# An attention block whose score mask and softmax division move to VectorE, beside a busy GpSimd

## What the reference computes

```python
s = scale * q @ k.T                     # 768 tokens: 512 latent, 256 context
s = where(|query - key| <= WINDOW or key is context, s, NEG_INF)   # latent queries; WINDOW = 128
m = max(s, sink);  p = exp(s - m);  p = p / (sum(p) + exp(sink - m))
o = p @ v                               # context queries see context keys only
```

## Time and profile before

| | us |
|---|---|
| median of 3 runs | 4390.55 |
| lowest and highest | 4390.1, 4399.13 |
| profiled execution, its own time | 4383.83 |
| span of the profiled execution | 4382.0 |
| PE busy | 3920.8 (89%) |
| DVE busy | 2531.0 (58%) |
| ACT busy | 1247.9 (28%) |
| POOL busy | 1195.2 (27%) |

### The profile page before, as it was taken

The page is one execution under the profiler, slowest core; times in us unless marked ns, Lnnn a source line. Parts: engine busy times, 40 slices in busy tenths (PEclk is TensorE's granted clock), DMA queues, the critical chain, the costliest instruction groups (busy, mean ns, idle before and its releaser), DMA issues. The chain is left out here.

```text
span 4382.0 us, 53813 instructions
## 1 busy us (share of the span) xinstructions
PE 3920.8 (89%) x19828; PEld 2818.8 (64%) x19828; DVE 2531.0 (58%) x4600; ACT 1247.9 (28%) x2782; POOL 1195.2 (27%) x1458
## 2 busy tenths in 40 slices
PE   7899899989889766898989998989999789769998
PEld 4577455545445554777878885568855456668886
DVE  6634789972378884557668834245633309833353
ACT  3145311100212384663121102118711212341112
POOL 1174299950000068810000000049700011340000
PEclk9999999999999887999999999999999999889999
DMA  4542366542021056544335422124311176783221
GB/s 170 193 116 79 112 185 182 179 161 65 30 77 58 16 185 175 115 97 156 123 135 173 152 79 77 58 60 118 92 58 58 39 262 215 226 238 119 77 87 68
DMA packets 291090, 532.59 MB, mean 122 GB/s; under 512 B 181040, under 2 KB 187696, under 8 KB 266544
## 3 DMA queue, kind: packets, MB, share of 16 engines
q1 hardware_dynamic: 220080, 343.46, 24.1%
q0 software_dynamic: 53088, 180.65, 13.8%
q10 hardware_dynamic: 17696, 5.56, 0.6%
HBM read 429.42 MB, written 100.01 MB: 121 GB/s over the span
## 5 line engine op out<-in xcount | busy, mean ns | idle before, releaser
L409 PE MATMUL P<-hu,ring 128*128 128x384 f32 (+1 forms) x2448 | 745.8, 458 | 20.0 <-PEq L171 11.8
L409 PEld LDWEIGHTS P<-hu,ring 128*128 128x128 f32 x2448 | 466.6, 191 | 274.9 <-issue 22.6
L646 PE MATMUL P<-area,ring 128*128 128x256 f32 (+1 forms) x1880 | 493.1, 419 | 50.4 <-PEq L385 30.1
L646 PEld LDWEIGHTS P<-area,ring 128*128 128x128 f32 x1880 | 361.9, 194 | 170.9 <-issue 67.0
L409 PE MATMUL P<-area,ring 128*128 128x256 f32 (+1 forms) x1584 | 443.1, 432 | 3.5 <-DVE area L537 2.8
L866 POOL TENSOR_TENSOR fold<-mod,vec 128x16 f32<-128x16 f32 (+1 forms) x5 | 1.0, 206 | 1422.5 <-SPq L845 990.0
L409 PEld LDWEIGHTS P<-area,ring 128*128 128x128 f32 x1584 | 301.6, 191 | 127.5 <-issue 4.8
L646 PE MATMUL P<-area,hu 128*128 128x256 f32 (+1 forms) x1104 | 296.8, 423 | 0.0
L646 PEld LDWEIGHTS P<-area,hu 128*128 128x128 f32 x1104 | 209.7, 190 | 77.3 <-DVE hu L735 0.2
L2567 DVE SCALAR_TENSOR_TENSOR area<-area 128x1024 f32<-128x1024 f32 x122 | 222.2, 1821 | 17.8 <-ACT area L2643 15.7
L1077 DVE TENSOR_REDUCE stat<-P 128x1 f32<-128x512 f32 (+1 forms) x144 | 99.4, 690 | 151.2 <-PE P L996 92.8
(11 more groups left out here) (445 smaller groups left out, 7029.2 us busy)
## 6 DMA issues: line engine op xcount, KB each, us to landing
ring<-in_w_ffn_in SPq DMA_DIRECT2D x44, 1024.0 KB, 4.8
area<-in_w_mod SPq DMA_DIRECT2D x69, 512.0 KB, 3.3
ring<-s_c POOLq DMA_DIRECT2D x18, 1152.0 KB, 9.2
stat<-in_w_mod SPq DMA_DIRECT2D x39, 512.0 KB, 3.3
s_c<-area POOLq DMA_DIRECT2D x32, 576.0 KB, 3.3
ring<-in_w_ffn_out SPq DMA_DIRECT2D x24, 704.0 KB, 4.0
area<-s_b POOLq DMA_DIRECT2D x16, 1024.0 KB, 5.8
hu<-s_c POOLq DMA_DIRECT2D x14, 1152.0 KB, 9.0
```

The lines of the kernel that those rows point to most:

```text
L409: last = mm(to, col(a, k), b[:, k, :], start=fresh and k == 0, stop=k == q - 1, skip_group_check=True)
L646: last = mm(to, a[:, 128 * k:128 * k + 128], b[k], start=fresh and k == 0, stop=k == q - 1, skip_group_check=True)
```

## The change

In the windowed attention: the mask is no longer added by PE. It lies in tile stat as two ready rows of 640 and 512 columns, loaded by two DMAs instead of one, and DVE waits for them instead of PE. For t < 4, `peak` becomes a tensor_tensor_reduce, which adds the mask to the scores in place in PSUM and gives the maximum. `weigh` moves from ACT to DVE (a tensor_scalar with the reciprocal as a per-partition operand, from SBUF to SBUF), and `keep` from DVE to ACT. The other attention keeps its forms.

```diff
-    mask = c.view(at, 3 * 128) if window else None
+    masks = (c.stat[:, 1, 0:640], c.stat[:, 0, 128:640]) if window else None
...
-                sp.dma_start(mask, c.ins["window_mask"]).then_inc(sem["const"], 16)
+                sp.dma_start(masks[0], c.ins["window_mask"][:, 0:640]).then_inc(sem["const"], 16)
+                sp.dma_start(masks[1], c.ins["window_mask"][:, 640:1152]).then_inc(sem["const"], 16)
...
         def _(pe):
-            if window:
-                pe.wait_ge(sem["const"], 16)
...
-                    if key < LAT:
-                        for x in edges:
-                            to, of = a + 128 * (x - tiles[0]), 128 * (x - t + 1)
-                            last = nc.tensor.matmul(S[n % 2][:, to:to + 128], c.ident[:, :], mask[:, of:of + 128], start=False,
-                                                    stop=x == edges[-1], skip_group_check=True)
...
+            def keep(n):
+
+                i, j, t, _ = units[n]
+                act.wait_ge(sem["o"], n + 1)
+                nc.scalar.activation(out(i, j, t), O[n % 2], ACT.Copy).then_inc(sem["ocopied"], 1)
...
+            if window:
+                dve.wait_ge(sem["const"], 32)
...
-                nc.vector.reduce_max(small[:, n % slots, 0:1], scores(n), AX.X).then_inc(sem["top"], 1)
+                if window and t < 4:
+                    banned = masks[1] if t == 3 else masks[0][:, 128 if t == 0 else 0:640]
+                    nc.vector.tensor_tensor_reduce(scores(n), scores(n), banned, 1.0, -3e38, ALU.add, ALU.max,
+                                                   small[:, n % slots, 0:1]).then_inc(sem["top"], 1)
+                else:
+                    nc.vector.reduce_max(small[:, n % slots, 0:1], scores(n), AX.X).then_inc(sem["top"], 1)
...
+            def weigh(n):
+
+                dve.wait_ge(sem["inv"], n + 1)
+                p = prob[n % slots][:, 0:width(n)]
+                nc.vector.tensor_scalar(p, p, small[:, n % slots, 6:7], None, ALU.mult).then_inc(sem["unit"], 1)
...
                 if 1 <= n <= U:
                     finish(n - 1)
-                if n >= ahead:
+                    if window:
+                        weigh(n - 1)
+                if n >= ahead and not window:
                     keep(n - ahead)
```

More of the change, by code:

```diff
@@ L986, in score @@
                 i, j, t, tiles = units[n]
-                edges = [x for x in tiles if window and x < 4 and x != t and t < 4]
                 if n >= 2:
@@ L993, in score @@
                     last = nc.tensor.matmul(S[n % 2][:, a:b], q(i, j, t), k(i, j, key, key + b - a), start=True,
-                                            stop=rope is None and not (edges and key < LAT), skip_group_check=window)
+                                            stop=rope is None, skip_group_check=window)
                     if rope:
                         last = nc.tensor.matmul(S[n % 2][:, a:b], rope[0](i, t), rope[1][j][:, key:key + b - a], start=False, stop=True)
-                    if key < LAT:
-                        for x in edges:
-                            to, of = a + 128 * (x - tiles[0]), 128 * (x - t + 1)
-                            last = nc.tensor.matmul(S[n % 2][:, to:to + 128], c.ident[:, :], mask[:, of:of + 128], start=False,
-                                                    stop=x == edges[-1], skip_group_check=True)
                 last.then_inc(sem["score"], 1)
@@ L1056, in weigh @@
                 nc.scalar.activation(p, p, ACT.Copy, scale=small[:, n % slots, 6:7]).then_inc(sem["unit"], 1)
-            for n in range(U + ahead - 1):
-                if n >= ahead - 1:
+            def keep(n):
+                i, j, t, _ = units[n]
+                act.wait_ge(sem["o"], n + 1)
+                nc.scalar.activation(out(i, j, t), O[n % 2], ACT.Copy).then_inc(sem["ocopied"], 1)
+            for n in range(U + ahead):
+                if 0 <= n - ahead + 1 < U:
                     copy(n - ahead + 1)
@@ L1061, in _ @@
                     exps(n)
-                if 1 <= n <= U:
+                if window:
+                    if n >= ahead:
+                        keep(n - ahead)
+                elif 1 <= n <= U:
                     weigh(n - 1)
@@ L1069, in _ @@
                 dve.wait_ge(sem["sinks"], 1)
+            if window:
+                dve.wait_ge(sem["const"], 32)
             def peak(n):
-                i, j = units[n][0:2]
+                i, j, t, _ = units[n]
                 dve.wait_ge(sem["score"], n + 1)
@@ L3311, in constants @@
     a, b = i[:, None], i[None, :]
-    out["window_mask"] = np.concatenate([np.where(b >= a, 0, -1e30), np.zeros((128, 128)), np.where(b <= a, 0, -1e30)], 1)
+    before, after, open_ = np.where(b >= a, 0, -1e30), np.where(b <= a, 0, -1e30), np.zeros((128, 128))
+    out["window_mask"] = np.concatenate([before, open_, after, open_, open_, before, open_, open_, open_], 1)
     out["s5_same"] = (i[:, None] % 16 == np.arange(16)[None, :])
```

## The result

The changed kernel takes 4427.23 us (median of 4 runs, 4423.61 to 4432.56) against 4390.33 us: 1.0074 times the time before, 95% interval 1.006 to 1.0089, so 26 to 39 us slower. The two medians lie 36.9 us apart; the ratio, from the comparison of the single runs, is 32 us. The forecast was 4429 us. Its profiled execution has a span of 4421.5 us, 39.5 us more than before.

What follows compares the result with a forecast made beforehand. PE bounded the kernel before, POOL close behind; DVE would bound it while POOL works. The attention's 269 us meant +32, small terms +6, so 4390.55 + 38 = 4429 us; range 4400 to 4468.

Steps and rivals of the forecast that it cites:

- The fused maximum at the plain one's price: DVE's mask-adding maximum keeps its rows within 60 ns of 825 and 691, adding only an accumulator read.
- The accumulator's read: Extra read after DVE's fused maximum, taken as 82 ns, or 0.055 us a unit.
- Rival 4: DVE's fused maximum runs at half rate, 3.15 us a unit: +54 us and the small terms, 4450 us; chance 0.10.
- The division's own price: Division on DVE, SBUF to SBUF, without waits: 0.52 ns a column, 0.465 us for the mean of 469 columns.
- That it waits for GpSimd: The division on DVE waits for POOL's SBUF instructions, even three in a row; instructions reading PSUM are spared.
- rival 1: The division on DVE does not wait for POOL: 5 to 7 us gained, 4384 us; chance 0.10.
- How long: Division's wait for POOL: 1.05 us a unit, ends 0.38 and 1.78, making DVE's unit 2.75 us.
- Rivals 2 and 3: Division's waits short, 0.38 us (0 to +19 us, chance 0.15), or long, 1.78 us (+68 us, chance 0.10).
- GpSimd's delay: Divisions hold up POOL's table work by 0.3 us a unit, ending it after 255 us with 91 units done.
- The small terms: In the attention, waits in lumps of up to 5 us (+4 us) and a lower granted PE clock (+2 us).
- The signs: Expected in the attention's profile: DVE over 95% busy until POOL ends, no longer waiting for L991, block end near 3206.
- GpSimd's length as the floor: The attention block keeps POOL's length, 228 us of work plus its last store's landing, even with everything else free.

Runs made afterwards that it cites:

- tables_behind_before: Kernel before, with GpSimd's table work moved to its own block behind the attention: attention block 237.8 us, whole time 4632.2 us (one run).
- tables_behind_after: Changed kernel, with GpSimd's table work moved to its own block behind the attention: attention block 205.6 us, whole time 4599.9 us (one run).
- after_gap: Changed kernel, with GpSimd also waiting on a semaphore after each triple's first product in this block's tables: 4404.1 us, ratio 1.002.
- mask_alone: Changed kernel with the division back on ScalarE and the result's copy back on VectorE, leaving only the mask's part: 4392.6 us, ratio 0.9998.
- mask_sp_tables: mask_alone with the table work's DMAs issued by SyncE instead of GpSimd: 4379.0 us, ratio 0.9965.

## Why the prediction was right, and where it was not

- **What bounded it.** PE before, DVE after while GpSimd works, shown by the busy shares and by tables_behind_before and tables_behind_after.
- **The fused maximum at the plain one's price.** Right, 826 against 825 ns and 690 against 691. The accumulator's read is 138 ns, not 82: 0.04 us a unit more than its term. Rival 4 is out.
- **The division's own price.** 0.465 us forecast; (0.553 + 0.486 + 0.353) / 3 = 0.464 in tables_behind_after.
- **That it waits for GpSimd.** Right; rival 1 is out. The Trainium skill's section "Who interferes with whom" of "SBUF — State Buffer" says that VectorE contends with GpSimd in its two-port modes, which copy and tensor_scalar can enter, and does not with at most one SBUF input outside of them. The traces agree: divisions wait (1.56 us on average beside GpSimd, 0.46 behind it), copies from PSUM (at most 826 ns) do not. That the waiting side can be passed over was in no term of the forecast; after_gap shows a semaphore against it to be worth 21 us.
- **How long.** 1.05 us forecast. Measured (131.8 - 96 x 0.465) / 80 = 1.09 us over the 80 contended ones, a unit (3169 - 2942) / 80 = 2.84 us against 2.75. Rivals 2 and 3 are out.
- **The term that was mis-sized: GpSimd's delay.** I gave it 0.3 us a unit, so that its work would end after 255 us with 91 units done. Its last issue came 232.5 us after its first, against 227.5 before: 5 us, 0.06 us a unit. So 80 units were done by then, not 91, and 16 were left, not 5. The stretch from 3169 to the next block is 34.7 us, which less 3 us for the last values leaves 1.98 us for each of the 16, against 2.12 forecast. With the measured 0.06 in it, my own sum would have given 233 + 13 x 2.12 + 3 = 264 us; the longer unit, 2.84 us, then adds to it and the shorter one at the end takes off. That 269 stood so near the measured 267.3 (from GpSimd's first issue on) is in part luck: the misses cancel. The forecast of GpSimd's last issue at 3185 was wrong, it was 3168.9.
- **The small terms** for lumps and clock, +6 us together, do not show: the block grew by 30.0 us, less than the 32 of the sum without them. The clock did fall to 0.95 while GpSimd worked, from 0.98. Lumps may be a part of the 0.09 us by which a unit was longer; no run tells. That the median came out within 2 us of 4429 is luck too: by the block alone it would be 4420 to 4421, and the interval, 26 to 39 us, holds both this and the 36.9 us of the medians, so that time outside the block is not shown to be the change's.
- **The signs.** DVE was busy 94% until GpSimd ended, not over 95%, and still waited for L991, 9 times and 4.6 us in all. The block's end at 3203.7, near the 3206 forecast, is that of a block that began 5.6 us later than before.
- **GpSimd's length as the floor.** I took the block to end 2 or 3 us behind GpSimd's last store, and gave a free division 5 to 7 us of gain. mask_alone shows 8.5 us behind the last issue and no gain at all.

## What to carry to other kernels

Before moving an elementwise pass to VectorE, look at what GpSimd does in that stretch and at where the pass reads and writes: here the fast pass of 256 to 640 columns from SBUF to SBUF waited for GpSimd's instructions whole, and the passes that read PSUM did not, so try the PSUM passes on VectorE and the SBUF ones on ScalarE first. If such a pass must stay, break up GpSimd's back-to-back instructions with a semaphore, or issue its DMAs elsewhere: either took most of the loss away (247 and 227 us instead of 268), but neither made this change pay, and the two together were not run. And when one engine's part of a block shrinks, check which other end the block has before counting the gain.

## What the runs showed of the hardware that I had not expected

- A division that waits for GpSimd can be passed over by GpSimd's next instruction: 4.32 us for 0.35 us of work above. This happened to all 13 that began in a first product directly behind a DMA issue and to none of 7 whose product stood behind a wait. With a semaphore wait between all of GpSimd's instructions the longest row fell from 5.78 to 3.32 us.
- GpSimd itself loses next to nothing in the exchange: 5 us over 80 divisions.
- Instructions of one column, also from SBUF to SBUF, never waited for it: 211 to 217 ns for all 96 of L1091.
- Where the table work ends with a DMA that GpSimd issued, and nothing else comes later, the block ends 8.5 us behind the end of that issue (3159.04 to 3167.53 in mask_alone, 3372.63 to 3381.09 in tables_behind_after), of which a drain of GpSimd is 6.18 us in both. With the DMAs issued by SyncE the block ended with PE (mask_sp_tables, 219.6 us instead of 237.6).
